# Moving the Fourier transforms of both layers into the recurrence's woven work, and joining the tokens tile by tile on DVE

## The reference, cut to what matters

```python
def fourier_mix(u):                       # u: tokens x 256, four groups of 64 columns
    uh = split_heads(u, FT_GROUPS).astype(jnp.float32)
    y = jnp.fft.fft2(uh, axes=(1, 3), norm="ortho").real
    return y.reshape(u.shape).astype(u.dtype)

yl = jnp.concatenate([hgrn_out(ol_f + ol_b, pl[2]), diff_out(od_l).astype(hl.dtype),
                      fourier_mix(pl[8])], axis=-1) @ w_out
```

## Time and profile before

| quantity | value |
|---|---|
| runs, device time | 3156.93, 3159.25, 3161.83 us |
| profiled execution, first to last instruction (its span) | 3152.5 us |
| profiled execution's own device time | not in the page; the three runs stand 4.4 to 9.3 us above the span |
| PE busy | 2894.6 us, 92% of the span |
| DVE, ACT, POOL busy | 1617.8, 1033.2, 192.1 us |
| mean granted TensorE clock | 0.965 of full speed |

### The profile page before, as it was taken

One profiled execution on the slowest core, in us unless ns is written; L12 is line 12 of the kernel. 1 busy time (PEld: TensorE's weight loads), 2 busy tenths in 40 slices (PEclk: granted clock), 3 DMA queues, 4 the chain that ended last, 5 costly groups with the idle time before them and its releaser, 6 DMA issues.

```text
span 3152.5 us, 44843 instructions
## 1 busy us (share of the span) xinstructions
PE 2894.6 (92%) x18762; PEld 2379.0 (75%) x18762; DVE 1617.8 (51%) x3363; ACT 1033.2 (33%) x2010; POOL 192.1 (6%) x240
## 2 busy tenths in 40 slices
PE   7988899999999999898799999999899897899998
PEld 6766688888976666687668888888666687578886
DVE  4333544444446355877763424333935677654444
ACT  3223333223344145344232212111415444332222
POOL 0000000000000100100000000000210245100001
PEclk9999999999999999899899999999999898999999
DMA  7434322222222210222512122121121110223231
GB/s 238 154 107 146 103 74 61 54 59 69 61 101 95 77 34 1 85 81 82 190 65 94 47 74 67 54 67 54 54 72 34 31 41 1 94 94 110 91 105 56
DMA packets 228404, 250.58 MB, mean 79 GB/s; under 512 B 5696, under 2 KB 193196, under 8 KB 226668
## 3 DMA queue, kind: packets, MB, share of 16 engines
q1 hardware_dynamic: 227296, 245.77, 24.4%
q0 software_dynamic: 576, 1.84, 0.3%
q10 hardware_dynamic: 332, 0.12, 0.0%
HBM read 236.43 MB, written 9.44 MB: 78 GB/s over the span
## 4 chain that ended last, share of the span: by engine, by line
PE 55%; DVE 8%; ACT 4%; issue 2%; DMA 1%; POOL 1%; POOLq 0%; SPq 0%; ACTq 0%; DVEq 0%
PE PS L2199 52%; PE PS L2203 2%; ACT AR L181 1%; ACT L176 1%; PE PS L2409 1%; DMA WR<-in_w_in 1%; DVE AR L3181 1%; ACT EX L181 1%; DVE AR L2922 0%; DVE EX L3168 0%; DVE AR L2938 0%; DMA WR<-in_w_mod 0%; ACT STAT L181 0%; POOL HT L3240 0%; DVE AR L2947 0%
## 5 line engine op out<-in xcount | busy, mean ns | idle before, releaser
L2199 PE MATMUL PS<-HI,WC 128*128 128x512 f32 (+2 forms) x1600 | 427.9, 353 | 0.6 <-DVE WC L3162 0.6
L2199 PE MATMUL PS<-AR 128*64 128x64 f32 (+7 forms) x3436 | 301.7, 269 | 63.1 <-ACT AR L181 25.0
L2199 PE MATMUL PS<-DW,DH 128*128 128x384 f32 (+1 forms) x1344 | 357.2, 348 | 0.9 <-DVE AR L2783 0.9
L181 ACT ACTIVATE AR<-PS 128x256 f32<-128x256 f32 (+4 forms) x389 | 165.8, 453 | 553.7 <-PE PS L2199 434.0
L2199 PEld LDWEIGHTS PS<-AR 128*64 128x64 f32 (+5 forms) x3436 | 253.7, 171 | 109.5 <-issue 33.8
L2199 PEld LDWEIGHTS PS<-HI,WC 128*128 128x128 f32 x1600 | 284.0, 189 | 42.5 <-DVE WC L3162 1.1
L2199 PE MATMUL PS<-LO,WC 128*128 128x512 f32 (+2 forms) x800 | 282.2, 353 | 0.0
L2199 PE MATMUL PS<-WR,HT 128*128 128x128 f32 (+2 forms) x1296 | 255.2, 355 | 11.6 <-ACT AR L181 5.8
L2199 PE MATMUL PS<-HT,WR 128*128 128x256 f32 (+1 forms) x928 | 257.2, 429 | 6.7 <-DMA WR<-in_w_in 3.1
L2199 PEld LDWEIGHTS PS<-DW,DH 128*128 128x128 f32 x1344 | 241.9, 192 | 9.7 <-issue 7.1
L2199 PEld LDWEIGHTS PS<-WR,HT 128*128 128x128 f32 x1296 | 193.9, 198 | 66.2 <-issue 41.7
(11 more groups left out here) (458 smaller groups left out, 4948.1 us busy)
## 6 DMA issues: line engine op xcount, KB each, us to landing
WR<-in_w_ffn_in SPq DMA_DIRECT2D x40, 1024.0 KB, 6.4
WR<-in_w_in_b SPq DMA_DIRECT2D x51, 512.0 KB, 6.0
WR<-in_w_mod SPq DMA_DIRECT2D x12, 2048.0 KB, 8.0
WR<-in_w_mod SPq DMA_DIRECT2D x24, 1024.0 KB, 5.5
WR<-in_w_ffn_out SPq DMA_DIRECT2D x22, 1024.0 KB, 4.9
WR<-in_w_in SPq DMA_DIRECT2D x40, 512.0 KB, 5.3
WR<-in_w_out SPq DMA_DIRECT2D x8, 2048.0 KB, 11.3
WR<-in_w_in SPq DMA_DIRECT2D x4, 2048.0 KB, 7.8
```

The lines of the kernel that those rows point to most:

```text
L181: return self.o.activation(out, in_, func, **kw)
L2199: mm = lambda o, l, r, start, stop: e.o.matmul(o, l, r, start=start, stop=stop, skip_group_check=True)
```

## The change

What changes in the program:

- U is gone; the second half of each W2 tile goes to FTT, transposed by a view, and the transforms later work in place there.
- There is no fence and no shared join behind the tiles. Each tile's join is planned right behind its group, always on DVE, and waits for that group. The four swaps on POOL wait for the six joins and the transposes.
- The first weights of `project(0)` are loaded in the W2 loop, at tile 1, and two steps of `filling` (one group of 8 matmuls with 512 columns) are planned after the fence, ahead of the attention; `due` starts at -1.
- The transforms are a generator `transform`, the last link of `flow`, and so come behind the projections of head 3. It begins once head 1 has ended, whose buffers it uses: the whole of `k_dft` goes to X[:, 0:3584] and XC[:, 0:512] (1792 KB and 256 KB), PQ is XC[:, 512:1536], and `k_dftc` (512 KB) goes over the first table when its last product is done. Its PSUM banks are those of `flow` (`hturn`), its copies are all on ACT and held back by a step.

```diff
             for i in range(6):
-                both_parts = [(DV[:, i, :], 0, 256), (U[:, i, :], 256, 512)][:2 if i < nt else 1]
-                tok_split(i, W2, 512 if i < nt else 256, th, both_parts, eng_of(i))
+                o = [(DV[:, i, :], bk_cols(0, 256)), (FTT[:, :, 128 * i:128 * i + 128], bk_cols(256, 512, 2))][:2 if i < nt else 1]
+                p = tok_split(i, W2, 512 if i < nt else 256, th, o, eng_of(i))
+                cols = slice(128 * i, 128 * i + 128)
+                other = LTs[l][:, :, cols] if i < 4 else LXs[l][:, :, 128 * (i - 4):128 * (i - 4) + 128]
+                P.add("rj", HT3[:, :, cols], HDs[l][:, :, cols].bitcast(F32), other.bitcast(F32), [("pj", p.n)])
                 if i == 0:
                     late()
-            need = (("pj", P.count["pj1"]),)
-            fence()
-            for ks in (slice(0, 4), slice(4, 8)):
...
-            th = [("rj", P.count["rj"] + P.count["rj_d"])]
+                if i == 1:
+                    w = load([(128 * j, 128, w2[:, c:c + 128]) for j, c in enumerate((1536, 2048, 0))], 8, 384)
+                    first_w = [Chunk(w.slot, w.view[:, :, 128 * j:128 * j + 128], w.ready, w.until, ()) for j in range(3)]
+            th = [("rj", P.count["rj"])]
+            turned = [("qturn_" + e, turn_counts["q" + e]) for e in "ad"]
             for a in (0, 64):
-                (two swaps, waiting for th)
+                (two swaps, waiting for th + turned)
-            (the transforms, lines 1703 to 1723)
             fence()
@@
+            def transform(ring=hturn, heads=heads, set_until=set_until, both=both, FTT=FTT):
+                while not heads[1].ended:
+                    yield
+                until, owed = set_until[1], []
+                def settle():
+                    if owed:
+                        j, p, points = owed.pop()
+                        proj_copies(p)
+                        ring.done(j, *p.done)
+                        points += p.done
+                def one(n, pairs, w, need, to, free):
+                    settle()
+                    while ring.full():
+                        yield
+                    j, bk, b_until = ring.take()
+                    points = []
+                    for p in proj(bk[:, 0:n], pairs, w, need, b_until, [("a", to, bk[:, 0:n], None)], free, hold=True):
+                        if n == 512:
+                            yield
+                    owed.append((j, p, points))
+                    yield
+                    return points
+                PQ, free = [XC[:, 512:1024], XC[:, 1024:1536]], until
+                w = tables("k_dft", [X[:, 0:3584], XC[:, 0:512]], until)
+                rows = [X[:, 512 * k:512 * k + 512] for k in range(7)] + [XC[:, 0:512]]
+                for name, n, off in (("k_dft", T, 0), ("k_dftc", TC, 512))[:2 if both else 1]:
+                    kt = n // 128
+                    if off:
+                        w, rows = tables(name, [X[:, 0:1024]], stage_one), [X[:, 256 * k:256 * k + 256] for k in range(4)]
+                    for f in range(2):
+                        ready = []
+                        for c in range(2):
+                            pairs = [(FTT[:, f, off + 128 * k:off + 128 * k + 128], rows[kt * c + k]) for k in range(kt)]
+                            ready.append((yield from one(n, pairs, w, [], PQ[c][:, 0:n], free)))
+                        stage_one = (("pj", P.count["pj1"]),)
+                        settle()
+                        yield
+                        yield from one(n, [(cs64[:, 128 * c:128 * c + 128], PQ[c][:, 0:n]) for c in range(2)], None, ready[0] + ready[1],
+                                       FTT[:, f, off:off + n], ())
+                        free = (("pj", P.count["pj1"]),)
+                settle()
@@
-            due = [0]
+            due = [-1]
+            for _ in range(2):
+                next(filling)
@@
-            flow = itertools.chain(*[project(h, prr=hturn, slots=by_quarter, after=heads[0] if h == 3 else None) for h in (2, 3)])
+            flow = itertools.chain(*[project(h, prr=hturn, slots=by_quarter, after=heads[0] if h == 3 else None) for h in (2, 3)], transform())
@@
             carried_end()
-            for _ in mods:
+            for _ in itertools.chain(mods, flow):
                 pass
```

More of the change, by code:

```diff
@@ L1641, in tok_split @@
                 j, bk, until = lring.take()
-                p = proj_now(bk[:, 0:n], w.by_token(l, i, 0, n), w.ready, need, until, [(eng, o, bk[:, lo:hi], None) for o, lo, hi in to], free)
+                p = proj_now(bk[:, 0:n], w.by_token(l, i, 0, n), w.ready, need, until, [(eng, o, view(bk), None) for o, view in to], free)
                 lring.done(j, *p.done)
@@ L1698, in build @@
-            th = [("rj", P.count["rj"] + P.count["rj_d"])]
-            for a in (0, 64):
-                P.add("swap", QS[64 - a:128 - a, :, :], QKT[a:a + 64, 0:2, 0:512], th)
-                P.add("swap", KS[64 - a:128 - a, :, :], QKT[a:a + 64, 2:4, 384:768], th)
-            pq_until = ()
-            for who, (n, name, tiles0, off) in enumerate(((T, "k_dft", 0, 0), (TC, "k_dftc", 4, 512))):
-                if who and not both:
-                    continue
-                kt = n // 128
-                tabs = [load_flat(A[name][:, c * kt * n:(c + 1) * kt * n], kt * n) for c in range(2)]
-                ready = []
-                for c in range(2):
-                    v = k3(tabs[c].view, kt)
-                    for f in range(2):
-                        j, bk, until = lring.take()
-                        p = proj_now(bk[:, 0:n], [(U[:, tiles0 + k, 128 * f:128 * f + 128], v[:, k, :]) for k in range(kt)], tabs[c], [], until,
-                                     [(eng_of(f), PQ[:, c, f, 0:n], bk[:, 0:n], None)], pq_until)
-                        lring.done(j, *p.done)
-                        ready += p.done
-                for f in range(2):
-                    j, bk, until = tring.take()
-                    p = proj_now(bk[:, 0:n], [(cs64[:, 128 * c:128 * c + 128], PQ[:, c, f, 0:n]) for c in range(2)], None, ready, until,
-                                 [(eng_of(f), FTT[:, f, off:off + n], bk[:, 0:n], None)])
-                    tring.done(j, *p.done)
-                pq_until = (("pj", p.n),)
@@ new lines, in build @@
+                if i == 1:
[3 more added lines that the diff above has]
+            turned = [("qturn_" + e, turn_counts["q" + e]) for e in "ad"]
+            for a in (0, 64):
+                P.add("swap", QS[64 - a:128 - a, :, :], QKT[a:a + 64, 0:2, 0:512], th + turned)
+                P.add("swap", KS[64 - a:128 - a, :, :], QKT[a:a + 64, 2:4, 384:768], th + turned)
@@ L1751, in build @@
             spare_at = early.at
[L1752 removed]
+            prr, early_w = banks(6, 7), {0: first_w}
             hpair, hturn, hout = Ring(pair(0), pair(2)), banks(4, 6) if both else banks(4, 6, 7), banks(5)
@@ L1781, in weights @@
                     return ws[n] if n < 5 else None
-                if slots is None:
+                if slots is None and not ws:
                     w = load([(128 * j, 128, a) for j, a in enumerate(pieces(h)[:3])], 8, 384)
                     ws += [Chunk(w.slot, w.view[:, :, 128 * j:128 * j + 128], w.ready, w.until, ()) for j in range(3)]
-                else:
+                elif slots:
                     weights(1 if both else 2)
@@ L1885, in main, with tables @@
                 yield from recur(heads[h], ended)
+            def tables(name, to, until):
+                wloads["f"] += 16 * len(to)
+                at_, loads = 0, []
+                for a in to:
+                    loads.append((a, A[name][:, at_:at_ + a.shape[1]]))
+                    at_ += a.shape[1]
+                w = Chunk("f", None, ("wf", wloads["f"]), until, loads)
+                P.add("load", w)
+                return w
+            def transform(ring=hturn, heads=heads, set_until=set_until, both=both, FTT=FTT):
[39 more added lines that the diff above has]
+                settle()
@@ L3244, in swap @@
                 e.o.dma_start(to, src).then_inc(sem("swap"), 16)
-            return dict(fence=fence, rj=rj, swap=swap, hp2=hp2, hl1=hl1, hl2=hl2, g2=g2, an=an, dump=dumped(e))
+            return dict(fence=fence, swap=swap, hp2=hp2, hl1=hl1, hl2=hl2, g2=g2, an=an, dump=dumped(e))
         def sp_program(e):
```

24 lines of the change are left out of this document (6 added, 18 removed).

## The result

The kernel became slower: 3170.3 us, the median of five runs (3168.1 to 3177.6), against 3156.9 for the kernel before on the same chip, a ratio of 1.0053 (95% interval 1.0037 to 1.0069). The forecast was 3144, 0.5% faster, with 3130 to 3161 as range. It missed in sign and in size. Differences of a fifth of a per cent are told from the ratios and from stages of the profiles, as the executions of one kernel differ by up to 0.5%.

What follows compares the result with a forecast made beforehand. PE, busy 92% of the span, was taken as the bound. The terms -29.3 (tiles to attention), +9 and +4.7 (layer 0's and 1's recurrences) gave -15.6 us, so 3144 us by the median, range 3130 to 3161.

Steps and rivals of the forecast that it cites:

- The joins: Behind each W2 tile group: moved from POOL to DVE, about 1.2 us each, only the sixth on the path.
- The drain that ends with the landing: Behind the last tile: POOL's drain lasts until the swaps land, 7.2 us from its first issue.
- the moved products find idle time: Recurrence's second half: of 41.0 us of moved matmuls, most fall into PE idle time.
- Layer 1's back: Layer 1's recurrence: four fifths of 17.7 us of moved matmuls hide, 4.7 us exposed, no table wait.
- the front: Last W2 tile to attention: 17.1 us gained in layer 0 and 12.2 in layer 1, 29.3 in all.
- I carry 3 us: Layer 0's recurrence, head 2: PE waits 8 to 13 us for `k_dft`, mostly hidden, 3 us exposed.
- I take 6 us: Layer 0's recurrence, head 3: PE waits 4 to 6 us for `k_dftc`, and late `w_mod` chunks move the end; 6 us exposed.
- the table's wait: Slower rival, recurrence: PE stands at each table's first product, delaying DVE; 15 and 8 us exposed, 3167 us; chance 0.06.
- `due` at -1 puts one of the two steps back: Attention: starting the filling's counter at -1 holds back one early step; no effect priced.
- PE is idle for 8.8 us: Behind each layer's last tile: join, first issue, drain and semaphores leave PE idle 8.8 us, bounds 6.7 and 14.
- So group and scores take 6.3 us: After PE's idle gap: first projection group and attention scores, at the lower clock, take 6.3 us in each layer.
- Both signs: Named as showing it wrong: gain between tiles and attention under 20 us, or DVE waiting for PE in heads 2 and 3.

Runs made afterwards that it cites:

- part 1: Two kernels: the changed kernel with the `k_dft` table asked for earlier, 3162.1 us, and with `k_dftc` asked for earlier too, 3152.8 us.
- part 6: `due` started at 0: in the changed kernel, 3158.0 us; with early tables and late fence too, 3126.1 us, or 3120.7 with 0 in layer 0 alone.
- fence_late: The changed kernel with the fence behind the swaps moved behind the two early projection steps: 3150.1 us, ratio 0.9982.
- all_three_due0: The changed kernel with both tables asked for earlier, the fence behind the early steps, and `due` at 0 in layer 0, -1 in layer 1: 3120.7 us.
- all_three_due0_act: As `all_three_due0`, with the four swap DMAs per layer issued on ACT's queue and not POOL's: 3118.3 us, ratio 0.9879.
- no_transform: The changed kernel without any transform, so tables, products and copies are left out in both layers: 3145.2 us, ratio 0.9962.

## Why the prediction was wrong

**Right.** The joins: 1.22 us each on DVE. The drain that ends with the landing: 1070.0 and 1069.8 us again. The Trainium skill (Perfetto Trace Analysis, DMA Instruction, SWDGE (GPSIMD)) says when the record of the DMA itself ends, with its descriptors and not with the data. The trace agrees: the four records took 2.5 us in all and the landings 5.5 to 6.5; the drain behind them is another instruction, and it waited. That the moved products find idle time: exposed beside the waits were 0.7 and 0 us by the stages, 7.6 in all by the medians. Layer 1's back came to +1.4 for the forecast's 4.7, with no table wait. And scores and first steps were done 20.0 us behind the tile, against 32.3 before, with one step more in the 20.0: the front's work was done sooner, but the gain didn't last to the end of the attention.

**Wrong, by its own steps.**

*"I carry 3 us" and "I take 6 us" for the table waits of layer 0.* This is the largest single term of the miss, 9.7 us. PE stood for 10.3 us, in the middle of the 8 to 13 that the forecast gave, and for 6.7, just over its 4 to 6. The error was in what hides them. The argument was that DVE's next unit has its products 12 us ahead, that DVE waits for PE only once, and that PE was idle there anyway. The second was read short: two waits for the modulation, one of 4.1 us, stand beside the 2.3. DVE had 7.3 us of work left, not 12, and then waited 10.0 us for PE: the wait lies in PE's in-order queue ahead of the transposes that DVE needs next, whatever idle time PE had later. The two waits cost 8.0 and 10.7 us (part 1), 18.7 for the 9. So the case that held was "the table's wait", which had 0.06 and a threshold of 12 us. There is no such threshold at 12: 10.3 us cost 8.0. Its sum was wrong too. It adds 15 + 8 = 23 to a forecast that has 9 us for the same two waits in it; without counting them twice it is -29.3 + 23 + 4.7 = -1.6, or 3158 and not 3167. So no case of the list led, by its own terms, to a kernel slower by this wait alone.

*"`due` at -1 puts one of the two steps back, which moves nothing that I can price."* It moved 15.1 us in layer 0's attention and 7.3 the other way in layer 1's (part 6). The forecast let the attention be "the same work" and gave the early steps their PE time back. Layer 0 gave nothing: 202.5 to 202.9 us with a group of PE's less in it. The window before, to be read against the first one of part 6:

```profile
1082.76:1285.30 202.54, 178.57 (x912) 125.19 (x912) 111.55 (x257) 98.14 (x218) 3.65 (x2) 0.94 0.08 22
```

PE is busy 5.9 us less after the change and idle 6.2 us more (24.0 to 30.2). Of the 10.6 us by which layer 0's front gained less than its 17.1, 4.9 are lost by the end of the first scores, and 5.7 here.

*"PE is idle for 8.8 us."* 10.5 and 11.0: the landings took 5.5 to 6.5 and 6.0 to 7.4 us, and POOL's first issue came 1.9 us behind the tile, not 1.5. The forecast took the landings of layer 0 and held that what ran beside them was "now elsewhere". Layer 1's longest landing fell from 8.3 us to 7.4 without the tables, but layer 0's rose from 5.1 to 6.5, with the 1024 KB of weights named above beside it. This mis-sizes a term by 1.7 and 2.2 us.

*"So group and scores take 6.3 us."* The row of 3.70 us and x8 is one step, half of a group; the two steps are x16 and took 8.6 and 10.1 us, begun at the low clock, where `fence_late` shows 7.1 at the high one. In the forecast the second half had no time at all, which makes 3.1 and 4.7 us. With the longer gap, this is why layer 1 had its scores no earlier than before and gained 5.6 us, all in the attention, for 12.2.

Together: the front -12.1 for -29.3, the back +22.7 for +13.7, and 5.7 us of stretches that the change doesn't touch: 16.3 of the 16.4 us between the two spans. So of the 32 us between forecast and span the front as a whole has 17, the back 9 and those stretches 6. Both signs that the forecast had named for being wrong came: the front gained under 20 us, and DVE began to wait for PE. The moved work itself is not what cost. With the tables asked for in time, the fence behind the early steps and `due` per layer the changed kernel is faster than the one before by 36 us (`all_three_due0`) or 38 (`all_three_due0_act`, 3118.3 us). How much of this the moved transforms bring is not parted: `all_three_due0` has also gained from `due` in the attention, and no run has the best fence and `due` with the transforms in their old place.

Open is why an attention is shorter by 15 us with one start of `due` and longer by 7 in the other layer; that it hangs on where the steps fall is shown, and for layer 0 the waits for ACT that go; a rule that gives the best start is not. Open is also where 6 of the 7.6 us of `no_transform` lie, and why its recurrences, with neither products nor table waits, are still 2.0 and 1.3 us longer than those of the kernel before.

## What to carry to other kernels

When work is moved into another engine's idle time, first ask when its operands are asked for: 41 us of matmuls cost there between 0.7 us by the stages and 7.6 by the medians, and two loads planned one step ahead of their first use cost 18.7 us, since idle time that comes later in an in-order queue doesn't hide a wait that stands ahead of it. Work pulled ahead to cover a wait belongs ahead of the fence that makes the wait, where it also finds the clock still high: the same two steps were worth 20 us more there than behind it. And a counter that shifts a woven schedule by one step is an edit like any other: it was worth 15 us in one direction and 7 in the other, and can only be tried.

## What was not expected of the hardware

- A drain on POOL, behind DMAs that POOL had issued, lasted until they landed (7.3 and 8.1 us); on ACT, behind the same four DMAs, it lasted 0.4 us and ended at least 3.6 us before the last of them landed. ACT took 4.2 us for the four issues against POOL's 2.5, since one of them took 2.1 us; the median issue was 0.68 us against 0.59.
- The same 16 records of matmuls took 7.1 us right behind the tiles' work, 8.6 and 10.1 us after idle gaps of 10.5 and 11.0 us, and 9.2 after one of 6.0.
- 23.3 us of products more, in the same 93 us of a recurrence, made PE busy for only 15.4 us more: the mean granted clock was 0.98 and not 0.85.
- The last stretch, which no edit touches, took 448.4 to 454.8 us in the profiled executions of the seventeen kernels: 448.4 to 449.4 in five, 451.6 or 451.7 in five, 454.6 to 454.8 in seven, with PE busy for 427.3, 430.5 and 433.7 us in one of each kind. What decides between them isn't shown. One execution doesn't tell a difference of 0.2%.
